# Two attention cores: the second head's probabilities are scaled on GpSimd, the first head's on VectorE

## The chip, the cores and the metric

The kernel runs on one core of one Trainium2 chip. The metric is the time of one execution on the device in microseconds (us). Engines are named as in the profile: PE is TensorE, DVE is VectorE, ACT is ScalarE, POOL is GpSimd, SP issues most of the transfers.

## The reference, cut to what matters

The program is two transformer stacks of two layers each on 256 tokens of width 1024, all in float32. Two of the four mixers are softmax attentions, and they alone are touched in what they compute with:

```python
def _sink_softmax(scores, sink):                 # first stack, layer 1: 16 heads, 256 queries, 512 keys
    m = max(sink, scores)                        # per query
    ex = [exp(s - m) for s in scores]
    denom = exp(sink - m) + sum(ex)
    return [e / denom for e in ex]               # then weights @ v

# second stack, layer 0 (mla_mixer): 16 heads, causal, 96-wide queries and keys, 64-wide values
    s = (qn . kn + qr . kr) * scale ; s = where(causal, s, MASK_VALUE)
    o = softmax(s) @ v
```

## The kernel before, in words

Each engine has its own instruction stream; semaphores tie them together. The streams are generated by one function, with one block for each engine. `stop >= 3` marks the first attention, `stop >= 5` the second, and both run through functions named `attention` (PE line 1120, DVE line 2305, ACT line 3059).

The first attention has 16 steps. Step n handles two heads (j = 0, 1) of one block of 128 queries: its scores are two banks of 128x512. The second attention has 8 steps of two heads; for each head there are 384 score columns, 256 for the later query block and 128 for the earlier one.

For step n the order is this. PE `score` writes two banks. DVE `most` masks them in place, takes the row maximum (line 2370, or 2495 and 2496) and makes the bias of the exponential. ACT `weights` makes the exponentials into `a_prob[:, n % 3, j, :]` with their row sums. DVE `normed` adds the sink's part (first attention only), takes the reciprocal of the sums (lines 2378, 2502) and scales the probabilities of both heads in place (helper `scale`, line 1788: one instruction for each head in the first attention, two for each head in the second), then raises `att_normed`. PE `turns_of` transposes the probabilities, head by head, into PS[0] and PS[1] (helper at line 646; 4 transposes a head, or 3). ACT copies each to SBUF (`att_copied`). PE `weigh` multiplies them with the values (line 1222, or 1330), and DVE copies the result out (line 2317, `att_taken`).

The steps are pipelined by hand. On PE, iteration s holds score(s), turns(s-2), weigh(s-3), in that order. On DVE it holds most(s), normed(s-1), the copy of s-3. On ACT it holds weights(s) and the two copies of s-1. PE line 1129 waits for `att_normed` before the turns of both heads.

GpSimd does nothing in either attention. Its stream goes from the sums of down-projection weights (line 3414) straight to a memset for the delta-rule mixer (line 3417). Two one-off semaphores of that mixer, `g_end_ready` (raised once, line 2572) and `g_half` (raised twice, line 2632), order VectorE's results before their readers on PE and ACT.

Of the kernel before, what the change touches and what calls it, by code (L numbers as in the profile page):

```python
# [106 lines left out]
def build(nc, A, out, stop=99):  # L107
    ctx = ExitStack()
    with ctx:
# [101 lines left out]
        for name in (  # L211
            "const_loaded", "vectors_loaded", "x_loaded", "phase_loaded", "rows_loaded", "packs_turned", "packs_copied",
            "cond_ready", "x_turned", "x_copied", "panel_used", "ada_ready", "ada_taken", "final_scaled",
            "square_ready", "sum_ready", "mean_ready", "rstd_ready", "scaled", "h_ready",
            "gu_ready", "silu_ready", "gu_taken", "out_ready", "out_taken", "proj_ready", "proj_taken",
            "dve_step", "act_step", "pool_step",
            "act_for_dve", "dve_for_act", "act_for_pe", "dve_for_pe", "pe_for_dve",
            "gates_split", "moved_ready", "moved_taken", "picks_ready", "most_ready", "acc_ready", "acc_step", "out_stored",
            "strip_exped", "strip_made", "mix_rows_made", "mix_rows_stored", "floor_cleared", "floor_moved", "mix_cols_ready",
            "mix_masked", "mix_exped", "unit_scored", "unit_weighed", "unit_valued", "num_taken", "ret_squared", "ret_summed",  # L220
            "den_ready", "y_spread", "y_scaled", "y_ready", "y_squared", "y_gated", "y_summed",
            "att_scored", "att_maxed", "att_exped", "att_normed", "att_turned", "att_copied", "att_out", "att_taken",
            "norm_squared", "norm_added", "norm_inverted", "norm_rooted", "norm_spread",
            "g_rows_ready", "g_stored", "g_spread", "g_masked", "g_decayed", "g_cols_turned", "g_cols_ready", "g_end_ready", "g_summed", "g_logs", "g_grown", "g_keyed",
            "g_paired", "g_compact", "g_level_masked", "g_turned", "g_u", "g_u_copied", "g_w", "g_diag", "g_half", "g_inverted",
            "g_tok_turned", "g_tok_copied", "scan_ready", "scan_u0", "scan_s", "scan_r", "scan_u1", "scan_out", "scan_squared",
            "g_scaled", "g_final_turned", "g_final",
            "tok_turned", "tok_copied", "sum_cleared",
            "blk_tokens", "blk_sums", "blk_act", "blk_copied", "blk_ready", "blk_taken", "blk_silu",
            "down_tokens", "down_sums", "down_first", "down_copied", "down_ready", "down_taken", "down_added",  # L230
            "final_copied",
            "att_rooted", "att_scaled", "rot_ready", "rot_taken", "heads_copied",
        ):
            s[name] = ctx.enter_context(nc.semaphore(name))
        mix_loaded = [ctx.enter_context(nc.semaphore(f"mix_loaded{i}")) for i in range(16)]
# [393 lines left out]
        def _(pe):  # L629
# [490 lines left out]
            def attention(N, first, score, turns_of, weigh):  # L1120

                for step in range(N + 3):
                    if step < N:
                        if step >= 2:
                            pe.wait_ge(s["att_exped"], first + step - 1)
                        score(step, 4 + 2 * (step % 2)).then_inc(s["att_scored"], 1)
                    if 0 <= step - 2 < N:
                        n = step - 2
                        pe.wait_ge(s["att_normed"], first + n + 1)
                        for j in range(2):  # L1130
                            if n:
                                pe.wait_ge(s["att_copied"], 2 * (first + n - 1) + j + 1)
                            turns_of(n, j, PS[j]).then_inc(s["att_turned"], 1)
                    if step - 3 >= 0:
                        n = step - 3
                        pe.wait_ge(s["att_copied"], 2 * (first + n + 1))
                        if n >= 2:
                            pe.wait_ge(s["att_taken"], first + n - 1)
                        weigh(n, PS[2 + n % 2]).then_inc(s["att_out"], 1)
# [202 lines left out]
            if stop >= 7:  # L1342
# [39 lines left out]
                for h in range(8):  # L1382
                    if h == 0:
                        pe.wait_ge(s["act_step"], 1 + 24)
                    elif h == 3:
                        pe.wait_ge(s["g_end_ready"], 1)
                    elif h in (4, 5):
                        pe.wait_ge(s["proj_taken"], c["proj"].n - 1)
                    elif h >= 6:
                        pe.wait_ge(s["g_paired"], h - 3)  # L1390
                    bank = PS[KEY_BANKS[h]]
                    for t in range(2):
                        v = slice(t * P, (t + 1) * P)
                        last = nc.tensor.matmul(bank[:, t * L:(t + 1) * L].rearrange("p (a n) -> p a n", a=2), g_x[:, 8 + h, v],
                                                g_x[:, h:h + 9:8, v], start=True, stop=True)
                    last.then_inc(s["g_keyed"], 1)
# [78 lines left out]
                    last.then_inc(s["g_w"], 1)  # L1475
                for g in range(2):
                    pe.wait_ge(s["g_diag"], g + 1)
                    pe.wait_ge(s["g_half"], g + 1)
                    for m in range(8 * g, 8 * g + 8):
                        last = product(PS[U_BANKS[g]], slice(64, P), m, g_pair[0:64, m // 2, m % 2, 1, 64:P], g_t1[0:64, m, :], 64)  # L1480
                    last.then_inc(s["g_u"], 1)
# [18 lines left out]
                for g in range(2):  # L1500
                    heads = range(4 * g, 4 * g + 4)
                    whole = lambda h: PS[h % 4]
                    outs = lambda h: PS[4 + 2 * g + h % 4 // 2][:, h % 2 * L:h % 2 * L + L]
                    pe.wait_ge(s["g_inverted"], g + 1)
                    for h in heads:
                        nc.tensor.matmul(whole(h)[:, 0:P], g_tt[:, 2 * h, :], g_v[:, h, 0, :], start=True, stop=True)\
                            .then_inc(s["scan_ready"], 1)
# [260 lines left out]
        def _(dve):  # L1768
# [4 lines left out]
            def link(ins):  # L1773

                ins.then_inc(s["dve_step"], 1)
                dve.wait_ge(s["dve_step"], c["step"].next())
# [9 lines left out]
            def scale(o, i, by, plus=None, op1=ALU.add):  # L1786
                if plus is None:
                    return V.tensor_scalar(o, i, by, None, ALU.mult)  # L1788
                return V.tensor_scalar(o, i, by, plus, ALU.mult, op1)
# [529 lines left out]
            if stop >= 3:  # L2319
# [54 lines left out]
                def normed(n):  # L2374

                    pair = slice(2 * n, 2 * n + 2)
                    link(tt(dsum[:, pair], dsum[:, pair], esink[:, pair], ALU.add))
                    link(V.reciprocal(rec[:, pair], dsum[:, pair]))
                    for j in range(2):
                        v = a_prob[:, n % 3, j, :]  # L2380
                        last = scale(v, v, rec[:, 2 * n + j:2 * n + j + 1])
                    return last

                attention(16, 0, most, normed, P, lambda n: hT[:, n // 2, (n % 2) * P:(n % 2 + 1) * P])
                add_project_out(1, 1, 5)
# [4 lines left out]
            if stop >= 5:  # L2390
# [108 lines left out]
                def normed_m(n):  # L2499

                    four = slice(4 * n, 4 * n + 4)
                    link(V.reciprocal(rec[:, four], dsum[:, four]))
                    for j in range(2):
                        for i, v in ((j, a_prob[:, n % 3, j, 0:L]), (2 + j, a_prob[:, n % 3, j, L:L + P])):
                            last = scale(v, v, rec[:, 4 * n + i:4 * n + i + 1])
                    return last

                attention(8, 16, most_m, normed_m, L, lambda n: hT[:, n, 0:L])
# [5 lines left out]
            if stop >= 7:  # L2514
# [54 lines left out]
                        V.tensor_copy(gcols, PS[7][:, 0:56]).then_inc(s["g_cols_ready"], 1)  # L2569
                dve.wait_ge(s["g_cols_turned"], 2)  # L2570
                dve.wait_ge(s["g_cols_ready"], 1)
                tt(small[:, G_DECAY:G_DECAY + 8], PS[7][:, 64:72], small[:, G_BIAS:G_BIAS + 8], ALU.add).then_inc(s["g_end_ready"], 1)

                def copy_gate(half, t):

# [49 lines left out]
                for g in range(2):  # L2625
                    dve.wait_ge(s["g_w"], 8 + g + 1)
                    bank = of(PS[W_BANKS[g]])
                    scale(group(g_t1, g)[32:64, :, 0:32], bank[32:64], -1.0)
                    for p in range(2):
                        r = slice(64 * p, 64 * p + 32)  # L2630
                        last = scale(group(g_tt, g)[r, :, 64 * p + 32:64 * p + 64], bank[r], -1.0)
                    last.then_inc(s["g_half"], 1)
                for g in range(2):
                    dve.wait_ge(s["g_w"], 10 + g + 1)
                    scale(group(g_tt, g)[0:64, :, 64:P], PS[W_BANKS[g]][0:64, :].rearrange("p (m n) -> p m n", m=8), -1.0)\
# [183 lines left out]
        def _(act):  # L2819
# [352 lines left out]
            if stop >= 7:  # L3172
# [19 lines left out]
                for b in range(24 + 2):  # L3192
# [10 lines left out]
                    if 3 <= b < 19:  # L3203
                        act.wait_ge(s["act_step"], c["step"].n - 1)
                        ac(g_sq[:, b - 3, :], g_x[:, b - 3, :], ACT.Square).then_inc(s["square_ready"], 1)
                act.wait_ge(s["g_end_ready"], 1)
                ac(small[:, G_DECAY:G_DECAY + 8], small[:, G_DECAY:G_DECAY + 8], ACT.Exp)
                ac(small[:, G_GROWN:G_GROWN + 16], small[:, G_ROWS:G_ROWS + 16], ACT.Exp).then_inc(s["g_grown"], 1)
                for h in range(8):
# [163 lines left out]
        def _(pool):  # L3373
# [26 lines left out]
            for j in range(1, 4):  # L3400
# [11 lines left out]
                if j > 1:  # L3412
                    pool.wait_ge(s["down_taken"], 10 * (j - 2) + 8)
                G.tensor_tensor(down_s4, down_weights(wa, 1), down_s2, ALU.subtract).then_inc(s["down_sums"], 1)
            if stop >= 7:
                pool.wait_ge(s["g_rows_ready"], 1)
                nc.gpsimd.memset(g_tt.rearrange("p m n -> p (m n)"), 0.0).then_inc(s["pool_step"], 1)  # L3417
# [109 lines left out]
```

## Time and profile before

| | us |
|---|---|
| median of 3 runs | 2345.54 |
| lowest, highest | 2343.82, 2351.57 |
| profiled execution, its own time | 2345.32 |
| its span in the profile | 2343.5 |
| PE busy | 2249.6 (96%) |
| VectorE busy | 1053.6 (45%) |
| ScalarE busy | 435.1 (19%) |
| GpSimd busy | 109.4 (5%) |

Times in the rows are microseconds from the span's start, or durations. In a timeline, one row can be several instructions of one kind that overlap or follow each other (x2, x8), with their joint duration. In brackets stands how long the engine was idle before and what released it. "mem" is SBUF, "banks" is PSUM. In a table of groups the last columns are: busy us in all, mean ns of one instruction, idle us before them. The first attention runs from about 940 to 1001, the second from about 1345 to 1376.

### The profile page before, as it was taken

What the parts mean: (1) busy time and instruction counts of PE and PEld (TensorE: products, weight loads), DVE (VectorE), ACT (ScalarE), POOL (GpSimd) and SP (SyncE); (2) the same over time, 40 slices, a digit from 0 to 9 for tenths busy, and PEclk for the clock granted to TensorE, in tenths of its full rate; (3) what the DMA queues carried; (4) which work ended last, traced back from release to release, by engine and by line L of the source; (5) the groups of instructions that cost most, each with busy time, mean ns of one, the idle gap of its engine ahead of it and who ended that gap; (6) DMA issues with size and microseconds to landing.
All of it is one profiled execution on the core that took longest, in us unless ns stands there. A gap on an engine that the chain in (4) does not pass through costs nothing.

```text
span 2343.5 us, 38868 instructions
## 1 busy us (share of the span) xinstructions
PE 2249.6 (96%) x16734; PEld 1629.6 (70%) x16734; DVE 1053.6 (45%) x2019; ACT 435.1 (19%) x1023; POOL 109.4 (5%) x103
## 2 busy tenths in 40 slices
PE   6999999999999999899999999999998989999997
PEld 4444454478885887588888678888775876666665
DVE  4586464488886346834432655450334420000001
ACT  3211251100000012720001241000332321111101
POOL 0210210000001220000000000000003000000000
PEclk8999999999999999999999999999999989999999
DMA  9334522245445223038884426886532258888894
GB/s 352 133 123 158 175 69 72 72 149 200 155 156 148 74 93 133 1 130 294 294 244 137 144 73 236 294 262 164 183 123 95 73 189 301 326 323 324 325 337 172
DMA packets 306216, 428.13 MB, mean 183 GB/s; under 512 B 11603, under 2 KB 166866, under 8 KB 305802
## 3 DMA queue, kind: packets, MB, share of 16 engines
q1 hardware_dynamic: 303412, 422.55, 52.9%
q10 hardware_dynamic: 2646, 3.26, 0.4%
q8 instruction: 125, 2.05, 0.4%
q14 instruction: 33, 0.27, 0.0%
HBM read 424.55 MB, written 1.13 MB: 182 GB/s over the span
## 4 chain that ended last, share of the span: by engine, by line
PE 90%; DVE 5%; ACT 2%; issue 1%; DMA 1%; SPq 1%; DVEq 0%; ACTq 0%
PE banks L637 76%; PE banks L891 3%; ACT mem L2821 2%; PE banks L646 1%; DVE mem L1795 1%; PE banks L1591 1%; PE banks L1000 1%; DVE mem L1788 1%; DVE mem L1792 1%; PE banks L1035 1%; DMA mem<-in_ada_w 1%; DVE mem L2370 1%; PE banks L1655 1%; PE banks L1422 1%; PE banks L855 1%
## 5 line engine op out<-in xcount | busy, mean ns | idle before, releaser
L637 PE MATMUL banks<-mem 128*32 128x128 f32 (+5 forms) x12660 | 1827.1, 360 | 22.9 <-ACT mem L2821 12.1
L637 PEld LDWEIGHTS banks<-mem 128*128 128x128 f32 (+3 forms) x12660 | 1309.4, 149 | 514.2 <-issue 312.2
L1792 DVE SCALAR_TENSOR_TENSOR mem<-mem 128x512 f32<-128x512 f32 (+5 forms) x509 | 366.6, 745 | 14.1 <-ACT mem L2821 4.5
L2821 ACT ACTIVATE mem<-banks 128x512 f32<-128x512 f32 (+8 forms) x367 | 145.9, 421 | 1126.3 <-PE banks L637 824.4
L2821 ACT ACTIVATE mem<-mem 128x256 f32<-128x256 f32 (+9 forms) x421 | 184.1, 490 | 662.3 <-DVE mem L1792 517.1
L1795 DVE TENSOR_TENSOR mem<-mem,banks 128x256 f32<-128x256 f32 (+3 forms) x88 | 43.1, 491 | 575.3 <-ACT mem L2821 548.7
L1792 DVE SCALAR_TENSOR_TENSOR mem<-banks,mem 128x256 f32<-128x256 f32 (+7 forms) x258 | 133.6, 543 | 341.5 <-PE banks L637 225.8
L1795 DVE TENSOR_TENSOR mem<-mem 128x256 f32<-128x256 f32 (+12 forms) x286 | 160.0, 569 | 36.2 <-ACT mem L2821 21.1
L1795 DVE TENSOR_TENSOR mem<-banks,mem 128x256 f32<-128x256 f32 (+3 forms) x223 | 90.5, 410 | 112.3 <-PE banks L637 61.4
L646 PE MATMUL banks<-mem 128*128 128x128 f32 (+3 forms) x396 | 64.0, 301 | 29.8 <-DMA mem<-in_ctx 11.3
L646 PEld LDWEIGHTS banks<-mem 128*128 128x128 f32 (+3 forms) x396 | 48.5, 155 | 57.2 <-issue 21.7
L891 PE MATMUL banks<-mem 128*128 128x256 f32 x320 | 75.6, 380 | 0.0
L2821 ACT ACTIVATE mem<-banks,mem 128x512 f32<-128x512 f32 (+4 forms) x110 | 55.3, 511 | 90.9 <-PE banks L637 59.8
L891 PEld LDWEIGHTS banks<-mem 128*128 128x128 f32 x320 | 60.9, 190 | 8.1
L2821 ACT ACT_TABLE_LOAD x41 | 52.6, 1283 | 25.3 <-issue 24.6
L3417 POOL MEMSET mem<- 128x2048 f32 x1 | 1.8, 1805 | 908.3 <-DVE mem L1792 908.3
L1792 DVE SCALAR_TENSOR_TENSOR mem<-mem,banks 128x256 f32<-128x256 f32 x88 | 35.3, 475 | 6.4 <-PE banks L735 6.4
L3407 POOL TENSOR_TENSOR mem<-mem 128x1408 f32<-128x1408 f32 x3 | 9.5, 3159 | 462.4 <-DMA mem<-in_ffn_w_out 418.7
L2328 DVE RECIPROCAL mem<-mem 128x512 f32<-128x512 f32 x6 | 20.1, 3352 | 22.6 <-ACT mem L2821 22.5
L3395 POOL TENSOR_TENSOR mem<-mem 128x256 f32<-128x256 f32 x32 | 22.6, 728 | 158.8 <-DMA mem<-mix_rows 158.6
L1000 PE MATMUL banks<-mem 64*128 64x256 f32 x192 | 27.0, 401 | 1.8 <-DVE mem L1792 1.6
L1591 PE MATMUL banks<-mem 128*128 128x192 f32 x128 | 25.8, 352 | 2.4 <-DVE mem L2745 2.4
(185 smaller groups left out, 820.9 us busy)
## 6 DMA issues: line engine op xcount, KB each, us to landing
mem<-in_ada_w SPq DMA_DIRECT2D x96, 1024.0 KB, 10.0
mem<-in_moe_w_gate_up SPq DMA_DIRECT2D x64, 1024.0 KB, 13.0
mem<-in_ffn_w_in SPq DMA_DIRECT2D x44, 1024.0 KB, 6.6
mem<-in_moe_w_down SPq DMA_DIRECT2D x48, 768.0 KB, 9.5
mem<-in_moe_w_gate_up SPq DMA_DIRECT2D x32, 768.0 KB, 12.7
mem<-in_ffn_w_out SPq DMA_DIRECT2D x32, 704.0 KB, 6.8
mem<-in_ffn_w_gate_up SPq DMA_DIRECT2D x22, 1024.0 KB, 6.7
mem<-in_ab_w_in SPq DMA_DIRECT2D x16, 1024.0 KB, 7.7
```

The lines of the kernel that those rows point to most:

```text
L637: ins = nc.tensor.matmul(o, lhsT, rhs, start=start, stop=stop)
L646: return nc.tensor.transpose(o, i, ident[0:n, 0:n])
L855: last = nc.tensor.matmul(bank, lhs[:, k, :], rhs[:, k, :], start=False, stop=k == KE_FF - 1, skip_group_check=True)
L891: last = nc.tensor.matmul(bank, a[:, k, :], b[:, k, :], start=False, stop=k == 3, skip_group_check=True)
L1000: last = nc.tensor.matmul(PS[2 * (n % 2) + j][:, i * L:(i + 1) * L], qk[r, first + 4 + p, key * P:(key + 1) * P], qk[r, first + p, q:q + L ...
L1035: nc.tensor.matmul(bank[j * HD:(j + 1) * HD, off + os.start:off + os.stop], mv[:, key, h * HD:(h + 1) * HD], mix_weights(h, u, d)[:, ws], ...
L1422: return nc.tensor.matmul(bank[into, (m % 8) * width:(m % 8 + 1) * width], lhsT, rhs, start=True, stop=True)
L1591: last = nc.tensor.matmul(bank[:, b * 2 * CAP:(b + 1) * 2 * CAP], h_tok[:, t, k * P:(k + 1) * P], pick[:, t, :], start=t == 0, stop=t == 1)
L1655: nc.tensor.matmul(moe_sum(4 * m + i), y_own[r, m, i % 2 * P:(i % 2 + 1) * P], back[r, e % 2, 0, :], start=False, stop=False, skip_group_c ...
L1792: return V.scalar_tensor_tensor(out=o, in0=a, scalar=sc, in1=b, op0=op0, op1=op1)
L1795: return V.tensor_tensor(o, a, b, op)
L2821: ac = lambda o, i, f, **k: nc.scalar.activation(o, i, f, **k)
```

## The change

The reciprocal of `normed` and `normed_m` raises a new semaphore `att_inverted`, on which both VectorE and GpSimd wait. VectorE then scales only head 0 and raises `att_normed`. GpSimd scales head 1 (one instruction of 128x512 a step in the first attention, one of 128x256 and one of 128x128 in the second) and raises a new semaphore `att_scaled_1`. PE waits for `att_normed` before the turns of head 0 and for `att_scaled_1` before those of head 1. To make room for two semaphores, `g_end_ready` becomes the second count of `g_cols_ready`, and `g_half` the first two counts of `g_inverted`.

```diff
@@ PE, attention @@
-                        pe.wait_ge(s["att_normed"], first + n + 1)
-                        for j in range(2):
+                        for j, scaled in enumerate(("att_normed", "att_scaled_1")):
+                            pe.wait_ge(s[scaled], first + n + 1)
                             if n:
                                 pe.wait_ge(s["att_copied"], 2 * (first + n - 1) + j + 1)
                             turns_of(n, j, PS[j]).then_inc(s["att_turned"], 1)
@@ DVE, normed @@
-                    link(V.reciprocal(rec[:, pair], dsum[:, pair]))
-                    for j in range(2):
-                        v = a_prob[:, n % 3, j, :]
-                        last = scale(v, v, rec[:, 2 * n + j:2 * n + j + 1])
-                    return last
+                    V.reciprocal(rec[:, pair], dsum[:, pair]).then_inc(s["att_inverted"], 1)
+                    dve.wait_ge(s["att_inverted"], n + 1)
+                    v = a_prob[:, n % 3, 0, :]
+                    return scale(v, v, rec[:, 2 * n:2 * n + 1])
@@ DVE, normed_m @@
-                    link(V.reciprocal(rec[:, four], dsum[:, four]))
-                    for j in range(2):
-                        for i, v in ((j, a_prob[:, n % 3, j, 0:L]), (2 + j, a_prob[:, n % 3, j, L:L + P])):
-                            last = scale(v, v, rec[:, 4 * n + i:4 * n + i + 1])
+                    V.reciprocal(rec[:, four], dsum[:, four]).then_inc(s["att_inverted"], 1)
+                    dve.wait_ge(s["att_inverted"], 16 + n + 1)
+                    for i, v in ((0, a_prob[:, n % 3, 0, 0:L]), (2, a_prob[:, n % 3, 0, L:L + P])):
+                        last = scale(v, v, rec[:, 4 * n + i:4 * n + i + 1])
                     return last
@@ POOL, before its work for the delta-rule mixer @@
+            if stop >= 3:
+                for n in range(16):
+                    pool.wait_ge(s["att_inverted"], n + 1)
+                    v = a_prob[:, n % 3, 1, :]
+                    G.tensor_scalar(v, v, a_mx[:, 4, 2 * n + 1:2 * n + 2], None, ALU.mult).then_inc(s["att_scaled_1"], 1)
+            if stop >= 5:
+                for n in range(8):
+                    pool.wait_ge(s["att_inverted"], 16 + n + 1)
+                    for i, v in ((1, a_prob[:, n % 3, 1, 0:L]), (3, a_prob[:, n % 3, 1, L:L + P])):
+                        last = G.tensor_scalar(v, v, a_mx[:, 4, 4 * n + i:4 * n + i + 1], None, ALU.mult)
+                    last.then_inc(s["att_scaled_1"], 1)
```

## Rows read from the trace of the kernel before

**Rows 1.** The page's head: the span of the profiled execution.

```profile
span 2343.5 us, 38868 instructions
```

**Rows 2.** Windows over the steady steps: busy, granted clock, DMA share, GB/s.

```profile
955.00:993.00 38.00, 35.68 (x315) 22.88 (x316) 36.06 (x103) 29.30 (x80) 0.00 (x0) 1.00 0.01 2
1357.00:1371.00 14.00, 12.82 (x90) 9.63 (x88) 13.55 (x47) 10.35 (x40) 0.00 (x0) 1.00 0.00 1
```

**Rows 3.** The chain that ended last, 957 to 962, its shares by line.

```profile
by line: DVE mem L1788 35.3%; DVE mem L2370 24.7%; DVE mem L1795 9.7%; DVE mem L2317 8.0%; DVE mem L2378 7.0%; DVE banks L1795 7.0%; DVE mem L1792 6.9%; issue 3.9%
```

**Rows 4.** Timelines of the first attention: start, duration, engine, instruction, idle before.

```profile
940.10 1.99 PE L1206 MATMUL banks<-mem 64*128 64x512 f32 x8
...
951.67 1.21 PE L646 MATMUL banks<-mem 128*128 128x128 f32 x8
951.79 0.43 DVE L1795 TENSOR_TENSOR banks<-banks,mem 128x256 f32<-128x256 f32 x1 [0.64 <-PE banks L1206]
...
954.18 0.88 DVE L1788 TENSOR_SCALAR mem<-mem 128x512 f32<-128x512 f32 x2
...
955.12 1.09 PE L646 MATMUL banks<-mem 128*128 128x128 f32 x8 [0.15 <-DVE mem L1788]
...
959.52 1.09 PE L1222 MATMUL banks<-mem 128*64 128x128 f32 x16
960.54 1.13 PE L1206 MATMUL banks<-mem 64*128 64x512 f32 x4
961.87 1.09 PE L646 MATMUL banks<-mem 128*128 128x128 f32 x8 [0.20 <-DVE mem L1788]
...
997.69 1.09 PE L646 MATMUL banks<-mem 128*128 128x128 f32 x8
```

**Rows 5.** Groups of instructions by form, 955 to 990: VectorE's scaling.

```profile
L1788 DVE TENSOR_SCALAR mem<-mem 128x512 f32<-128x512 f32 x21 | 9.3, 483 | 0.3
```

**Rows 6.** Timelines of the second attention.

```profile
1344.81 0.70 PE L1312 MATMUL banks<-mem 96*128 96x256 f32 x2 [0.84 <-DVEq L2485]
...
1346.22 0.60 PE L1312 MATMUL banks<-mem 96*128 96x256 f32 x2
...
1355.43 0.88 PE L646 MATMUL banks<-mem 128*128 128x128 f32 x6
...
1355.49 0.76 DVE L1795 TENSOR_TENSOR banks<-banks,mem 128x256 f32<-128x256 f32 x2
...
1357.03 0.70 PE L1312 MATMUL banks<-mem 96*128 96x256 f32 x2
...
1357.63 1.01 DVE L1788 TENSOR_SCALAR mem<-mem 128x256 f32<-128x256 f32 x4
...
1361.02 1.01 DVE L1788 TENSOR_SCALAR mem<-mem 128x256 f32<-128x256 f32 x4
```

**Rows 7.** Groups of instructions by form, GpSimd, the whole span.

```profile
L3423 POOL TENSOR_TENSOR mem<-mem 128x512 f32<-128x512 f32 x8 | 9.9, 1274 | 9.9 <-DMA mem<-decay_rows 9.9
...
L3442 POOL COPY mem<-mem 32x256 f32<-32x256 f32 x8 | 3.1, 394 | 0.3
L3417 POOL MEMSET mem<- 128x2048 f32 x1 | 1.8, 1805 | 908.3 <-DVE mem L1792 908.3
...
L3425 POOL MEMSET mem<- 128x1024 f32 x1 | 1.0, 951 | 1.0 <-ACT mem L2821 1.0
```

**Rows 8.** Timelines: VectorE and GpSimd beside each other, and alone.

```profile
55.62 10.34 DVE L1792 SCALAR_TENSOR_TENSOR mem<-mem 128x512 f32<-128x512 f32 x10
...
81.33 10.12 DVE L1792 SCALAR_TENSOR_TENSOR mem<-mem 128x512 f32<-128x512 f32 x14
...
1760.61 1.20 DVE L2581 TENSOR_SCALAR mem<-mem 128x8 f32<-128x8 f32 x1
...
1771.31 1.19 DVE L2594 COPY mem<-mem 32x256 f32<-32x256 f32 x4
...
1772.58 0.97 POOL L3431 TENSOR_TENSOR mem<-mem 128x256 f32<-128x256 f32 x1 [1.12 <-DVE mem L2594]
```

More of the change, by code:

```diff
@@ L223, in build @@
             "norm_squared", "norm_added", "norm_inverted", "norm_rooted", "norm_spread",
-            "g_rows_ready", "g_stored", "g_spread", "g_masked", "g_decayed", "g_cols_turned", "g_cols_ready", "g_end_ready", "g_summed", "g_logs", "g_grown", "g_keyed",
-            "g_paired", "g_compact", "g_level_masked", "g_turned", "g_u", "g_u_copied", "g_w", "g_diag", "g_half", "g_inverted",
+            "g_rows_ready", "g_stored", "g_spread", "g_masked", "g_decayed", "g_cols_turned", "g_cols_ready", "g_summed", "g_logs", "g_grown", "g_keyed",
+            "g_paired", "g_compact", "g_level_masked", "g_turned", "g_u", "g_u_copied", "g_w", "g_diag", "g_inverted",
             "g_tok_turned", "g_tok_copied", "scan_ready", "scan_u0", "scan_s", "scan_r", "scan_u1", "scan_out", "scan_squared",
@@ L231, in build @@
             "final_copied",
-            "att_rooted", "att_scaled", "rot_ready", "rot_taken", "heads_copied",
+            "att_rooted", "att_scaled", "rot_ready", "rot_taken", "heads_copied", "att_inverted", "att_scaled_1",
         ):
@@ L1385, in _ @@
                     elif h == 3:
-                        pe.wait_ge(s["g_end_ready"], 1)
+                        pe.wait_ge(s["g_cols_ready"], 2)
                     elif h in (4, 5):
@@ L1477, in _ @@
                     pe.wait_ge(s["g_diag"], g + 1)
-                    pe.wait_ge(s["g_half"], g + 1)
+                    pe.wait_ge(s["g_inverted"], g + 1)
                     for m in range(8 * g, 8 * g + 8):
@@ L1503, in _ @@
                     outs = lambda h: PS[4 + 2 * g + h % 4 // 2][:, h % 2 * L:h % 2 * L + L]
-                    pe.wait_ge(s["g_inverted"], g + 1)
+                    pe.wait_ge(s["g_inverted"], 2 + g + 1)
                     for h in heads:
@@ L2571, in _ @@
                 dve.wait_ge(s["g_cols_ready"], 1)
-                tt(small[:, G_DECAY:G_DECAY + 8], PS[7][:, 64:72], small[:, G_BIAS:G_BIAS + 8], ALU.add).then_inc(s["g_end_ready"], 1)
+                tt(small[:, G_DECAY:G_DECAY + 8], PS[7][:, 64:72], small[:, G_BIAS:G_BIAS + 8], ALU.add).then_inc(s["g_cols_ready"], 1)
                 def copy_gate(half, t):
@@ L2631, in _ @@
                         last = scale(group(g_tt, g)[r, :, 64 * p + 32:64 * p + 64], bank[r], -1.0)
-                    last.then_inc(s["g_half"], 1)
+                    last.then_inc(s["g_inverted"], 1)
                 for g in range(2):
@@ L3205, in _ @@
                         ac(g_sq[:, b - 3, :], g_x[:, b - 3, :], ACT.Square).then_inc(s["square_ready"], 1)
-                act.wait_ge(s["g_end_ready"], 1)
+                act.wait_ge(s["g_cols_ready"], 2)
                 ac(small[:, G_DECAY:G_DECAY + 8], small[:, G_DECAY:G_DECAY + 8], ACT.Exp)
```

## The prediction, made before the changed kernel was run

> **What bounds the kernel now.** I read the page first: a span of 2343.5 us [rows 1] in an execution of 2345.32, so 1.8 us lie around the span. Then I asked for the windows of the two attentions, because the change touches nothing else that takes time. In the steady steps of the first attention VectorE is busy 36.06 of 38 us and PE 35.68, in the second 13.55 and 12.82 of 14 [rows 2]. These are two engines at nearly the same load, so it matters which one ends each step. The chain of waits says it: between 957 and 962 every piece is VectorE's, 35.3% of it the scaling at line 1788 [rows 3]. PE stands idle for 0.20 us before the turns, released by that scaling; from 955.12 to 961.87 are two steps, 3.375 us each [rows 4]. The second attention has the same shape, 3.39 us a step (1357.63 to 1361.02) [rows 6]. The clock is at its upper level (1.00) in both windows and the DMA share 0.01 or less [rows 2]: no transfer is due, so the work behind an attention starts as much earlier as the attention ends earlier.
>
> **What is left when VectorE is relieved, first attention.** I call the start of PE's turns in iteration s T, and the start of VectorE's masking M.
> - PE alone: turns and weigh take 1.02 each (959.52 to 960.54 is one of them), a score 0.96 (two back to back take 1.99, of which some 0.07 is the pipeline's tail) [rows 4]. That is 3.00 us a step.
> - VectorE alone: 3.375 minus one scaling, which is 0.40 where two overlap (0.88 for two of 0.48) [rows 4, 5]: 2.98.
> - Across the engines, head 0: in the one iteration where VectorE waited for the scores, M is T + 0.12 (951.67, 951.79), the scaling begins 2.39 after M (954.18), takes 0.48, and PE starts 0.06 after the scaling's end (955.06, 955.12) [rows 4, 5]. So head 0 is ready at T + 3.05, and a step can't be shorter than 3.05.
> - Across the engines, head 1: GpSimd is released with VectorE by the reciprocal. The nearest row for its start is 0.08 after VectorE's end (1771.31 + 1.19 against 1772.58) [rows 8], while VectorE goes on 0.02 after its own reciprocal (its gaps are 3.9% of 5 us in the chain, some eight of them) [rows 3]; so VectorE's scaling goes first. If it keeps GpSimd out until it is done, GpSimd starts at M + 2.87 + 0.08. With X for its instruction and 0.06 to PE, head 1 is ready at T + 3.13 + X. Then PE has half the turns (0.51), a weigh (1.02) and a score (0.96) until the T two steps on. So two steps take 5.62 + X.
>
> **X, the price nobody has shown.** The trace has no tensor_scalar on GpSimd. Nearest is its one-input copy: 256 columns take 0.39, and a memset grows by 0.834 ns a column ((1805 - 951) / 1024) [rows 7]; for 512 columns 0.39 + 256 x 0.834 = 0.61. The far end is the two-input operation on the same 128x512: 1.27 [rows 7]. I take 0.61, since the scaling streams one tensor as the copy does; the operand of one column comes on top, unpriced. X = 0.61 gives 6.23 / 2 = 3.12 us a step, X = 1.27 gives 3.45. Below 0.48 head 0 bounds at 3.05. The step equals today's at X = 1.13.
> The Trainium skill (GPSIMD Engine Reference, section 3.1) gives 769 ns for 512 elements as the best case of a loop at 1.8 cycles an element; no run here shows it. By that figure a step would take 3.20 us and the 12 steps below would gain 2.1 in place of 3.1, an estimate from that page.
>
> **Sum, first attention.** M was bound to VectorE from 951.79 on, 12 steps of 3.375 until the last M at 992.3 [rows 4]. 12 x (3.375 - 3.12) = 3.1 us gained. At the end, the turns of the last step started at 997.69 [rows 4], 5.4 after the last M; now they start when turns(14) and one weigh are done. Head 1 of step 14 is ready at M + 3.0 + 0.61, its turns end at 4.1 and weigh(13) at 5.15: 0.2 gained. With X = 1.27 it is 12 x 0.07 = 0.8 lost, and 0.6 at the end. The first two steps lose nothing: there PE has a backlog at the lower clock level and finds both heads scaled. So +3.3, bounds -1.4 and (at 3.05) +4.3.
>
> **Second attention.** VectorE issues two scalings instead of four, 1.01 us for four [rows 6], so 0.46 to 0.50 less: about 2.93. PE: 1.60 for turns and weigh (1355.43 to 1357.03) and 1.41 for a score (1344.81 to 1346.22): 3.01 [rows 6]. GpSimd has 256 and 128 columns, 0.39 and 0.28, together 0.67 by the copy; by the two-input rate 0.73 and 0.46. Head 1: M is T + 0.06, the scaling starts at M + 2.14 [rows 6], two take 0.54, then 0.08 + 0.67 + 0.06: ready at T + 3.55; then 0.40 + 0.80 + 1.41, so 6.16 for two steps, 3.08 each. That would gain 0.31 a step.
> But here VectorE has a second scaling behind the first, and a waiting GpSimd may get in between. Then VectorE's second one waits 0.08 + 0.39, and the step is 3.40: nothing gained. Four steps are bound by VectorE in this way: 0 to 1.2 us. I take the middle, 0.6. At two-input rate without the intrusion it would gain 0.2, with it lose 4 x 0.35 = 1.4; the end adds 0 to -0.5.
>
> **What the trace says on sharing.** A VectorE tensor_scalar of 128x8 took 1.20 us beside GpSimd's 128x512 operations, though 128x512 takes 0.48 alone [rows 5, 8]: it waited for a whole GpSimd instruction. VectorE's two-input operations took 1.03 each beside GpSimd (10.34 for 10) and 0.72 alone (10.12 for 14) [rows 8]. The Trainium skill (SBUF — State Buffer, "Who interferes with whom") says that a tensor_scalar of VectorE in a 2-port mode and any GpSimd instruction exclude each other, whoever starts first. By that rule the trace's 1.20 agrees, and the two halves of the scaling would run one after the other and not together. My sum has it so by the row of 1.20; without any exclusion head 1 would be ready 0.5 earlier and head 0 would bound at 3.05.
>
> **The rest.** PE gains one wait for each step, behind which stand head 1's turns, the weigh and the next score: that is priced above. GpSimd waits in order from about 840 to 1373; behind it stands only the memset at line 3417, which was itself 908.3 us idle before [rows 7]. ScalarE copies each head when it is turned and is busy 29.30 of 38 [rows 2]. The merged semaphores add no instruction and keep the order of the same events: 0. Sum: 3.3 + 0.6 = 3.9 us; 2345.32 - 3.9 = 2341.4 for such an execution, and as the median stands 0.2 above the profiled one, 2341.6.
>
> **Rivals.**
> 1. GpSimd's scaling costs as much as its two-input work. This ends slower, from X = 1.13 on in the first attention: 1.4 lost there and between nothing and 1.9 in the second: 2347 to 2349. For it: an operand beside the stream. Against: one stream, and a copy at 0.39. Chance 0.25.
> 2. GpSimd gets the ports first, and VectorE's scaling waits for all of it. Head 0 is then ready at T + 0.12 + 2.37 + 0.08 + X + 0.54: 3.72 at X = 0.61, 4.38 at 1.27. 12 steps lose 4 to 12 us, the second attention 1 to 3: 2350 to 2361. For it: the 1.20 us row [rows 8]. Against: 0.02 against 0.08 us from release to start. Chance 0.10. (The Trainium skill, SBUF — State Buffer, "Who interferes with whom": whoever starts first holds the shared ports for its whole instruction; that rule would lead here if GpSimd started first.)
> 3. Dearer than any row, X near 2: 3.81 a step, 5.2 lost, 1 at the end, 3 in the second attention: 2355. Chance 0.07.
> 4. The engines hardly disturb each other: 3.05 in the first (3.9 + 0.4) and 3.01 in the second (4 x 0.38 + 0.3): 6.1 gained, 2339.4. This is as much as the change can give. Chance 0.07.
> 5. The steps get shorter and the kernel does not, because a later stage waits for its weights anyway: 2345.5. Against: DMA share 0.01 [rows 2]. Chance 0.03.
>
> **How the numbers follow.** The forecast has chance 0.48. A measurement of this kernel tells a change of 0.3%, 7 us, from none. No case gains 7 us: faster by more 0.02 (for what I have overlooked). Slower by more than 7 us are case 3 and the upper half of case 2, with a little of case 1: 0.10. Within: 0.88. The range holds the forecast and cases 1, 4 and 5, 0.83 together: 2339.4 to 2349, and I add 1 us at either end because three runs of the same kernel lay 1.7 below to 6 above their median: 2338.5 to 2350.
>
> **What would show it.** In the timeline the spacing of PE's turns: 3.12 (right), 3.375 or more (case 1), 3.7 and more with a VectorE scaling of over 1 us (case 2), 3.05 (case 4). GpSimd's rows give X and whether they start after VectorE's scaling ends. In the waits, PE's turns should be released by GpSimd and no longer by line 1788. In the second attention VectorE's second scaling shows whether GpSimd gets in between. The prediction is wrong if GpSimd's release takes much longer than 0.08 us, or if the wait moves to ScalarE.

## The result

| | median us | lowest, highest | runs |
|---|---|---|---|
| kernel before | 2347.32 | 2343.49, 2351.68 | 20 |
| changed kernel | 2351.38 | 2347.25, 2355.10 | 20 |

The changed kernel is slower: the ratio to the kernel before is 1.0017, with a 95% interval of 1.0011 to 1.0023, so 2.6 to 5.4 us. The forecast was 3.9 us faster. The profiled execution of the changed kernel took 2355.10 us, the slowest of its 20, with a span of 2353.3. Its span must not be subtracted from that of [rows 1]: 2.7 of the 9.8 us between them were already there when the first attention began (942.83 against 940.10), where the change does nothing. Another 2.0 lie between the two attentions (346.24 us against 344.20) and 2.4 behind the second (969.45 against 967.01). I put neither down to the change: over the eleven traces of this document these two stretches vary from 344.2 to 346.3 and from 966.7 to 971.5 us, and the one behind took 968.5 in a version in which GpSimd does nothing in the attentions (e7). What the change did is read inside the two attentions.

The page's head and its line of busy times; then windows over the same stretch as [rows 2] for the first attention and the matching one for the second (columns: us, PE, PEld, VectorE, ScalarE, GpSimd busy, granted clock, DMA share, GB/s):

```profile
span 2353.3 us, 38890 instructions
...
PE 2254.9 (96%) x16734; PEld 1628.7 (69%) x16734; DVE 1046.9 (44%) x1987; ACT 435.1 (18%) x1023; POOL 152.9 (6%) x135
```

```profile
955.00:993.00 38.00, 34.43 (x304) 21.49 (x304) 30.89 (x87) 27.85 (x74) 19.66 (x11) 1.00 0.01 1
1364.00:1378.00 14.00, 13.19 (x96) 9.79 (x92) 12.64 (x38) 10.79 (x41) 6.66 (x8) 1.00 0.00 1
```

VectorE was relieved as intended, from 36.06 to 30.89 us in the 38 of the first attention. But PE does less in the same time as well (35.68 to 34.43). A new wait has taken the place of the old one. The groups by form show the price of what was moved (last columns: busy us, mean ns of one, idle us before):

```profile
L3418 POOL TENSOR_SCALAR mem<-mem 128x512 f32<-128x512 f32 x16 | 29.7, 1857 | 133.3 <-DVE mem L2378 133.3
...
L3423 POOL TENSOR_SCALAR mem<-mem 128x256 f32<-128x256 f32 x8 | 8.7, 1084 | 365.6 <-DVE mem L2501 365.6
...
L3423 POOL TENSOR_SCALAR mem<-mem 128x128 f32<-128x128 f32 x8 | 4.8, 601 | 0.0
```

GpSimd's scaling takes 1.86 us. The two-input operation on the same shape, which the prediction took as the far end, takes 1.27 [rows 7]. The chain of waits, first its shares by line over 957 to 992, then one turn of the loop (start, length, what):

```profile
by line: POOL mem L3418 26.7%; DVE mem L2370 17.7%; PE banks L1206 15.5%; PE banks L1222 13.7%; PE banks L646 9.4%; DVE banks L1795 6.3%; issue 3.5%; DVE mem L1795 3.5%; DVE mem L2378 2.5%; DVE mem L1792 2.5%
...
962.13 0.66 PE banks L646 x4
962.78 1.02 PE banks L1222 x16
963.81 1.08 PE banks L1206 x4
...
964.91 0.44 DVE banks L1795
...
965.38 1.24 DVE mem L2370
...
966.84 0.24 DVE mem L1795 x2
...
967.10 0.18 DVE mem L2378
...
967.36 1.87 POOL mem L3418
...
969.27 0.66 PE banks L646 x4
```

In [rows 3] every piece is VectorE's. Here the chain goes from PE's turns of head 1 over the weigh and the score to VectorE's maximum and reciprocal, to GpSimd, and back to the turns of head 1 two steps later. That circle takes 7.14 us (962.13 to 969.27), where two steps took 6.75 in [rows 4]. PE shows it too: in the steps that close the circle, which is every second one, head 0 is turned at once and head 1 waits for GpSimd.

```profile
966.84 1.13 PE L1206 MATMUL banks<-mem 64*128 64x512 f32 x4
967.90 0.66 PE L646 MATMUL banks<-mem 128*128 128x128 f32 x4
969.27 0.66 PE L646 MATMUL banks<-mem 128*128 128x128 f32 x4 [0.71 <-POOL mem L3418]
969.86 1.09 PE L1222 MATMUL banks<-mem 128*64 128x128 f32 x16
970.88 1.13 PE L1206 MATMUL banks<-mem 64*128 64x512 f32 x4
971.94 1.09 PE L646 MATMUL banks<-mem 128*128 128x128 f32 x8
972.97 1.09 PE L1222 MATMUL banks<-mem 128*64 128x128 f32 x16
```

**Where the time is.** I cut each attention at PE's turns: the fill up to the fourth iteration's turns (at 951.67 in the kernel before, 953.55 in the changed one), the steady steps from there to the last turns that follow a score (992.26 and 996.49), and the tail up to the next projection.

| us, profiled executions | first: 12 steady steps | per step | tail | second: 4 steady steps | per step | tail |
|---|---|---|---|---|---|---|
| before | 40.59 | 3.38 | 8.35 | 13.42 | 3.36 | 7.64 |
| changed | 42.94 | 3.58 | 9.01 | 13.61 | 3.40 | 7.92 |

The sum is 2.35 + 0.66 + 0.19 + 0.28 = 3.5 us, inside the measured 2.6 to 5.4. The fill of the first attention went the other way in this pair of executions, 10.72 us against 11.57: PE's fourth score took 1.13 us, in the kernel before 2.08, at a granted clock of 0.50. This is not the change's doing. With GpSimd at work e1 has the short fill (10.72) and e8 the long one (11.58), and e7, in which GpSimd does nothing there, has 10.71. So I leave the fill out of the sum.

### The profile page after: what moved, and what is told of

Its sections match the earlier page's. It is cut to its first block, busy times and chain, and to the rows that moved or that the text cites. A ratio compares the mean times of both kernels' runs of the same rounds, so it can differ in the third digit from the quotient of the medians.

```text
span 2353.3 us, 38890 instructions
## 1 busy us (share of the span) xinstructions
PE 2254.9 (96%) x16734; PEld 1628.7 (69%) x16734; DVE 1046.9 (44%) x1987; ACT 435.1 (18%) x1023; POOL 152.9 (6%) x135
## 3 DMA queue, kind: packets, MB, share of 16 engines
q10 hardware_dynamic: 2646, 3.26, 0.4%
HBM read 424.55 MB, written 1.13 MB: 181 GB/s over the span
## 4 chain that ended last, share of the span: by engine, by line
PE 91%; DVE 4%; ACT 2%; issue 1%; DMA 1%; POOL 1%; SPq 1%; DVEq 0%; ACTq 0%
PE banks L637 76%; PE banks L891 3%; ACT mem L2820 1%; PE banks L646 1%; DVE mem L1795 1%; PE banks L1591 1%; PE banks L1000 1%; DMA mem<-in_ada_w 1%; DVE mem L1792 1%; PE banks L1035 1%; PE banks L1655 1%; PE banks L1422 1%; PE banks L855 1%; POOL mem L3418 1%; SPq L492 1%
## 5 line engine op out<-in xcount | busy, mean ns | idle before, releaser
L3418 POOL TENSOR_SCALAR mem<-mem 128x512 f32<-128x512 f32 x16 | 29.7, 1857 | 133.3 <-DVE mem L2378 133.3
L3423 POOL TENSOR_SCALAR mem<-mem 128x256 f32<-128x256 f32 (+1 forms) x16 | 13.3, 842 | 365.6 <-DVE mem L2501 365.6
```

The costliest lines, as they stand in the source:

```text
L3418: G.tensor_scalar(v, v, a_mx[:, 4, 2 * n + 1:2 * n + 2], None, ALU.mult).then_inc(s["att_scaled_1"], 1)
```

## The experiments

Each kernel ran on one chip together with the kernel before; "ratio" is to that, with its 95% interval. e1, e5 and e8 were executed once each, so only their traces are read. Steps, fill and tail are cut as above. The code is cut to the lines that matter and shows the first attention; the second has the matching edit.

**e1: GpSimd starts only after VectorE's scaling.** How much of 1.86 us is the instruction, how much is waiting for VectorE?

```diff
-                    pool.wait_ge(s["att_inverted"], n + 1)
+                    pool.wait_ge(s["att_normed"], n + 1)
```

> The changed kernel, but GpSimd waits until VectorE has scaled head 0 (att_normed) instead of for the reciprocal (att_inverted), so that the two scalings never overlap. In the changed kernel GpSimd's 128x512 scaling took 1.86 us from 0.06 after VectorE's start. Theory 1 (the instruction itself costs 1.86 us): it takes 1.86 again, starts 0.45 later, and two steps take 7.15 + 0.45 = 7.6 us. Rival (0.4 of the 1.86 is waiting for VectorE's scaling of 0.49): it takes 1.4 to 1.45, ends where it ended before, and two steps take 7.15 to 7.25 us.

```profile
L3418 POOL TENSOR_SCALAR mem<-mem 128x512 f32<-128x512 f32 x16 | 25.0, 1565 | 139.9 <-DVE mem L1788 139.9
```

Alone it takes 1.57 us, between the two expectations: 0.29 of the 1.86 is the overlap with VectorE, the rest is its own. For 256 and 128 columns it takes 926 and 605 ns here, so 2.5 ns for each column and 0.29 fixed. The steps took 3.69 us (3.58 in the changed kernel): GpSimd now starts 2.96 after VectorE's masking began, 0.51 later than in the changed kernel, and gets 0.29 of it back. Two steps took 7.39, between the 7.15 to 7.25 and the 7.6 expected. With this instruction, then, letting both start at once is right, and the price is what is wrong.

**e2: VectorE scales both heads.** Everything of the diff but GpSimd: does the split wait or the merging of semaphores cost anything?

```diff
-                    v = a_prob[:, n % 3, 0, :]
-                    return scale(v, v, rec[:, 2 * n:2 * n + 1])
+                    v = a_prob[:, n % 3, 0, :]
+                    scale(v, v, rec[:, 2 * n:2 * n + 1]).then_inc(s["att_normed"], 1)
+                    v = a_prob[:, n % 3, 1, :]
+                    return scale(v, v, rec[:, 2 * n + 1:2 * n + 2])      # raises att_scaled_1
```

> All of the change but GpSimd: VectorE scales both heads and raises att_normed after head 0 and att_scaled_1 after head 1; the split wait on PE and the merged semaphores stay. Theory 1 (the loss is GpSimd's chain and nothing else): steps of 3.375 us as before the change, ratio to the kernel before 0.9995 to 1.0000. Rival (the rest of the change costs the 1.5 us of the measured 4 that the two attentions don't show): ratio 1.0004 to 1.0010.

Measured: 2345.13 against 2347.50 us, ratio 0.9994 (0.9985 to 1.0003), steps of 3.35 and 3.30 us. The rest of the change (the split wait, the merged semaphores) costs nothing that can be measured, so the loss is GpSimd's part.

**e3: the weigh leaves the loop.** PE turns head 1 after the weigh of the step before, not ahead of it (the edit in words):

```diff
-    score(s); turns of head 0 of s-2; turns of head 1 of s-2; weigh(s-3)
+    score(s); turns of head 0 of s-2; weigh(s-3); turns of head 1 of s-2
```

> The changed kernel, but PE turns head 1 only after the weigh of the step before: score(s), turns of head 0 of s-2, weigh(s-3), turns of head 1 of s-2. Theory 1 (a loop over two steps through GpSimd, 4.5 us from T to head 1 ready and then half the turns, a weigh and a score): the weigh leaves the loop, which falls from 7.15 to 6.1 for two steps; PE itself bounds at 3.05 to 3.15 us a step; first attention 3 us shorter than before the change, second about 1.4 shorter, ratio to the kernel before 0.9978 to 0.9985. Rival (ScalarE, whose copy of head 1 now comes later and stands ahead of its next exponentials, becomes late): steps of 3.3 us and more, ratio 0.9995 to 1.0015.

```profile
965.26 1.13 PE L1210 MATMUL banks<-mem 64*128 64x512 f32 x4
966.32 0.66 PE L646 MATMUL banks<-mem 128*128 128x128 f32 x4
966.91 1.09 PE L1226 MATMUL banks<-mem 128*64 128x128 f32 x16
967.93 0.66 PE L646 MATMUL banks<-mem 128*128 128x128 f32 x4
968.52 1.13 PE L1210 MATMUL banks<-mem 64*128 64x512 f32 x4
...
by line: PE banks L646 35.8%; PE banks L1226 32.2%; PE banks L1210 32.0%
```

The last line is the chain of waits from 957 to 992: every piece of it is PE's. The same GpSimd instruction, still 1857 ns, no longer holds up a step. The step is 3.26 us and no row of PE has idle time ahead of it, so PE is the bound. That confirms the loop. I expected 3.05 to 3.15 and had set PE's floor too low for this order: two groups of turns take 0.59 each where one takes 1.02, and a score takes 1.06. The rival's ratio came true, 1.0001 (0.9992 to 1.0010), but not its mechanism, since PE waits neither for ScalarE nor for anything else. The trace says where the gain went: the steady steps gain 1.5 us in the first attention (39.09 against 40.59) and 0.9 in the second (12.54 against 13.42), and the two tails lose 1.0 and 0.6. The 0.7 us that are left are too few for the ratio to show.

**e4: the two-input form.** GpSimd multiplies with the column of reciprocals repeated along the row.

```diff
-                    G.tensor_scalar(v, v, a_mx[:, 4, 2 * n + 1:2 * n + 2], None, ALU.mult)
+                    G.tensor_tensor(v, v, a_mx[:, 4, 2 * n + 1:2 * n + 2].to_broadcast([P, T2]), ALU.mult)
```

> The changed kernel, but GpSimd scales with the two-input tensor_tensor, the second operand being the column of reciprocals repeated along the row. Theory 1 (price of the form of the instruction; the trace has 1.27 us for tensor_tensor on 128x512): it takes 1.27 to 1.3, two steps take 6.55 us, ratio to the kernel before 0.9993 to 1.0000. Rival (both forms cost the same beside VectorE, because waiting for the shared ports makes up the 1.86): 1.8 and more, ratio 1.001 or above.

The timeline of one step:

```profile
965.35 1.36 DVE L1788 TENSOR_SCALAR mem<-mem 128x512 f32<-128x512 f32 x1
965.40 1.04 POOL L3418 TENSOR_TENSOR mem<-mem 128x512 f32<-128x512 f32 x1 [2.82 <-DVE mem L2378]
...
966.77 1.09 PE L646 MATMUL banks<-mem 128*128 128x128 f32 x8 [0.68 <-DVE mem L1788]
```

Neither expectation held in its mechanism. The form is cheaper than any expected (1.04 us), and the kernel is the slowest of all: ratio 1.0043 (1.0028 to 1.0059), 3.84 us a step. VectorE's own scaling takes 1.36 us in place of 0.49. This is rival 2 of the prediction, in a form it did not foresee: VectorE starts 0.05 us before GpSimd and waits for it all the same. It ends 0.27 us after GpSimd. VectorE's streaming of 512 columns would take just that, at the 0.52 ns a column by which its group of 128x256 in the second attention (mean 350 ns) and that of 128x512 (483 [rows 5]) differ. So it looks as if VectorE had its fixed part behind it and streamed only when GpSimd was done; no row shows that directly.

**e5: both edits, two inputs and after VectorE.**

> Both edits of e1 and e4: GpSimd scales with the two-input form and starts only when VectorE has scaled head 0. Theory 2 (two separate prices: the form costs 1.04 us on GpSimd and 1.57 for tensor_scalar; and what overlaps pays extra, 0.29 on GpSimd's side for tensor_scalar, 0.87 on VectorE's side for the two-input form): VectorE's scaling is back at 0.49, GpSimd's stays 1.04, head 1 is ready 4.06 after VectorE's masking began, and with 2.68 for half the turns, a weigh and a score two steps take 6.75 us, 3.37 a step. Rival (the 1.04 of e4 was short because GpSimd held the ports from before VectorE, and the form costs 1.3 or more otherwise): 1.27 and more, 3.5 a step.

```profile
966.24 0.49 DVE L1788 TENSOR_SCALAR mem<-mem 128x512 f32<-128x512 f32 x1
...
966.80 1.04 POOL L3418 TENSOR_TENSOR mem<-mem 128x512 f32<-128x512 f32 x1 [2.44 <-DVE mem L1788]
```

VectorE's scaling is back at 0.49 and GpSimd's stays at 1.04: the price of the instruction and the obstruction are separate. The step is 3.42 us, close to the 3.37 expected and no better than the 3.38 before the change.

**e6: GpSimd takes half of head 1.** 256 of 512 columns in the first attention, the piece of 128 in the second; VectorE does the rest.

```diff
-                    v = a_prob[:, n % 3, 1, :]
+                    v = a_prob[:, n % 3, 1, 0:L]                          # GpSimd
+                    scale(v, v, rec[:, 2 * n:2 * n + 1]).then_inc(s["att_normed"], 1)
+                    v = a_prob[:, n % 3, 1, L:T2]                         # VectorE, after head 0
+                    return scale(v, v, rec[:, 2 * n + 1:2 * n + 2])
```

> The changed kernel, but GpSimd scales only half of head 1 in the first attention (256 of 512 columns) and only the 128-column piece of head 1 in the second; VectorE scales the rest after head 0, and the turns of head 1 wait for both. Theory 2 (the loop over two steps is GpSimd's price plus 5.2): GpSimd takes 1.1 to 1.25 for 256 columns, its loop falls to 3.2 a step, VectorE with 0.27 more is at 3.25 and sets the step; first attention 1.5 us shorter than before the change, second 0.5 to 1.0; ratio to the kernel before 0.9987 to 0.9996. Rival (VectorE's own scalings are held up by GpSimd's when there are several of them in a row, 0.77 instead of 0.54 for two in the second attention): VectorE's two take 1.0 and more in place of 0.75, steps of 3.38 to 3.5, ratio 1.0000 to 1.0010.

```profile
965.11 0.97 DVE L1790 TENSOR_SCALAR mem<-mem 128x512 f32<-128x512 f32 x2
965.17 1.22 POOL L3424 TENSOR_SCALAR mem<-mem 128x256 f32<-128x256 f32 x1 [2.25 <-DVE mem L2380]
...
L1790 DVE TENSOR_SCALAR mem<-mem 128x256 f32<-128x256 f32 x11 | 6.3, 570 | 0.0
```

GpSimd takes 1.22 us for 256 columns (0.93 alone, in e1, and 0.29), as expected. VectorE takes 0.97 for its two where 0.75 were due (0.40 and 0.35). It is the second that pays: 570 ns in place of 350, while its first keeps 488. So the rival was right: 3.45 us a step, ratio 1.0000 (0.9991 to 1.0009). In the second attention the step is 3.26, a little better than the 3.36 before.

**e7: relieve VectorE of something else.** No GpSimd; the split wait of e2; ScalarE copies each result out of PSUM.

```diff
-                        V.tensor_copy(place(n), PS[2 + n % 2][:, 0:width]).then_inc(s["att_taken"], 1)     # VectorE, n = step - 3
+                        ac(place(n), PS[2 + n % 2][:, 0:out_width], ACT.Copy).then_inc(s["att_taken"], 1)  # ScalarE, n = step - 3
```

> GpSimd does nothing, VectorE scales both heads with the split wait (as in e2), and the copy of each step's result out of PSUM (line 2317) goes from VectorE to ScalarE, between its exponentials and its copies of the turned heads. Theory 2 (what bounds the steps before the change is VectorE's 3.375 us, and what takes over is the loop M to head 1 to M two steps on, 3.27 + 0.06 + 3.0 = 6.35, or PE with 3.11): a step of 3.17 to 3.2 us in the first attention and about 3.1 in the second, 2.3 and 1.3 us less than before the change, ratio to the kernel before 0.9980 to 0.9988. Rival (ScalarE, busy 2.6 of 3.375 us a step and 0.3 more now, becomes late for the exponentials): steps of 3.3 and more, ratio 0.9995 or above.

```profile
966.92 0.88 DVE L1788 TENSOR_SCALAR mem<-mem 128x512 f32<-128x512 f32 x2
...
967.46 1.09 PE L646 MATMUL banks<-mem 128*128 128x128 f32 x8
967.72 0.43 DVE L1795 TENSOR_TENSOR banks<-banks,mem 128x256 f32<-128x256 f32 x1
...
by line: DVE mem L2366 38.8%; DVE mem L1788 27.7%; DVE banks L1795 11.1%; DVE mem L1795 8.1%; DVE mem L2374 5.6%; DVE mem L1792 5.4%; issue 3.7%
```

2342.82 against 2345.82 us, ratio 0.9987 (0.9978 to 0.9997): the one version here whose gain is clear of noise. The step is 3.18 us, and 3.07 in the second attention, as expected. The chain of waits from 957 to 992 (the last line) is still VectorE's throughout, but its step is 0.20 shorter; 0.03 of that is there without the moved copy (3.35 in e2).

**e8: a constant for the column.** Does the operand make GpSimd's tensor_scalar dear? As e1, but head 1 is multiplied by 0.5 and so not normalised.

> As e1 (GpSimd starts after VectorE's scaling, nothing overlaps), but GpSimd multiplies head 1 by the constant 0.5 in place of the column of reciprocals, so head 1 isn't normalised. Theory a (the operand that is a column of SBUF makes tensor_scalar dear): the 128x512 instruction falls from 1.57 us towards the copy's 0.61. Theory b (tensor_scalar on GpSimd costs 2.5 ns a column whatever its scalar is): 1.45 to 1.57 us.

```profile
L3418 POOL TENSOR_SCALAR mem<-mem 128x512 f32<-128x512 f32 x16 | 23.8, 1488 | 141.1 <-DVE mem L1788 141.1
```

1.49 us in place of 1.57: the column costs 0.08 and is not what makes the instruction dear. Why a tensor_scalar on GpSimd costs this much stays open.

**e9: the price that the prediction assumed.** GpSimd copies head 1 onto itself, with the waits of the changed kernel; head 1 is not normalised.

> The changed kernel with its own waits, but GpSimd copies head 1 onto itself and doesn't scale it, so head 1 isn't normalised. This gives the instruction the price that the prediction assumed. If that price was the only thing wrong in it: the copy takes 0.6 to 0.9 us, the loop through GpSimd falls to 3.0 to 3.1 a step, and the bound is head 0 or PE, 3.05 to 3.12 us a step in the first attention; 3.1 to 3.9 us less than before the change there, 0.5 to 1.5 less in the second; ratio to the kernel before 0.9978 to 0.9988. Rival (the two engines in each other's way cost as much as the price, as in e4, where VectorE's scaling took 1.36 in place of 0.49): VectorE's scaling of 0.8 us and more, steps of 3.3 us or more, ratio 0.9995 or above.

```profile
967.34 0.92 DVE L1788 TENSOR_SCALAR mem<-mem 128x512 f32<-128x512 f32 x1
967.37 0.61 POOL L3418 COPY mem<-mem 128x512 f32<-128x512 f32 x1 [2.80 <-DVE mem L2378]
...
968.32 1.09 PE L646 MATMUL banks<-mem 128*128 128x128 f32 x8 [0.24 <-DVE mem L1788]
...
1361.77 0.80 DVE L1788 TENSOR_SCALAR mem<-mem 128x256 f32<-128x256 f32 x2
1361.80 0.69 POOL L3423 COPY mem<-mem 128x256 f32<-128x256 f32 x2 [2.48 <-DVE mem L2501]
```

The copy takes 0.61 us, exactly the figure of the sum, and the kernel is not measurably faster: ratio 1.0003 (0.9995 to 1.0012), 3.40 us a step. VectorE's scaling takes 0.92 and ends 0.28 after GpSimd, as in e4. VectorE is the bound again, with 0.40 saved and 0.43 given back. So the price was not the only thing wrong. In the second attention (the last two rows) VectorE takes 0.80 where it took 1.01 [rows 6], and there the step falls from 3.36 to 3.18.

## Why the prediction was wrong

**What held.** VectorE was the bound, and its scaling released PE's turns [rows 3, 4]. The loop over two steps was the right structure, and so were its terms: VectorE's masking 0.11 after PE's turns begin (964.80 to 964.91), the scaling 2.39 after that (964.91 to 967.30 in the changed kernel), PE 0.04 after GpSimd's end. With X = 1.57 (e1) the sum's 5.62 + X gives 7.19 for two steps; measured 7.14. That this is so close is partly luck. The sum let GpSimd wait for all of VectorE's scaling and start 0.56 behind its start; it started 0.06 behind and took 0.29 longer for it. Half the turns took 0.58 where 0.51 stood and the score 1.06 where 0.96 stood, 0.17 more. The two errors nearly cancel. The merged semaphores and the split wait cost nothing measurable (e2). And the 3.5 us found inside the attentions leave nothing of size to a later stage.

**The step that failed: "X, the price nobody has shown".** It was put at 0.61 us by the nearest one-input row, with 1.27 as the far end. The instruction takes 1.57 alone and 1.86 in place. The argument "one stream, like the copy" was the fault: a copy and a multiplication by a scalar both stream one tensor, yet cost 0.83 (from 256 to 512 columns) and 2.5 ns a column on this engine (e9, e1). The two-input row was no bound either, since the two-input form is the cheaper one for this very work (1.04, e4). The break-even was named at X = 1.13, and rival 1, slower from X = 1.13 on, is the mechanism that decided, with its own price too small: it was bounded at 2349, and the measured median is 2351.38. Rival 3 came closest in price (X near 2, at 0.07).

**A second step would have failed as well: "VectorE's scaling goes first".** It was read from start times, 0.02 us against 0.08. In the changed kernel it came true by the instruction chosen: VectorE keeps its 0.49 and GpSimd pays 0.29. With a copy (e9) or the two-input form (e4) VectorE's row starts first too, by 0.03 to 0.05 us, and VectorE then ends after GpSimd's whole instruction. Rival 2 had the right consequence (its estimate of 3.72 us a step at X = 0.61 was 3.40 in e9, because VectorE streams only 0.27 after GpSimd and not all of 0.48 anew) and the wrong condition. Had X been 0.61, the 3.9 us would still not have come: in the trace of e9 the steady steps of the first attention gain nothing (40.76 us against 40.59), and the second attention gains 0.7 in its steps and 0.2 in its tail.

The Trainium skill (SBUF — State Buffer, "Who interferes with whom") says that whoever issues first has the shared ports for its whole instruction, and that the other is blocked for so long. In e4 and e9 the runs agree that VectorE's one scaling lasts until GpSimd's whole instruction is over, and differ on the order, if a row's start is taken for the issue: the engine whose row starts first is the one that waits. What a row gives as the start need not be the moment when the ports are taken, and I did not find out when that is. Where GpSimd's tensor_scalar meets the second of two VectorE scalings, the wait is not for a whole instruction: in e6 the second one takes 0.57 in place of 0.35 and is over at 966.08, while GpSimd works until 966.39.

**The range.** It reached 2350.0, from cases that bounded X at 1.27, and it was laid around a median of three runs, 2345.54; over 20 runs the kernel before has 2347.32. Both errors point the same way. A loss of 3.5 to 4.1 us on the first base is 2349.0 to 2349.6 and would have lain inside; on 2347.32 it doesn't. There is a slip in the chances as well: case 3 and the upper half of case 2 are 0.12, where 0.10 was put for them.

**The second attention.** The prediction had 0 to 1.2 us gained, depending on whether GpSimd gets between VectorE's two scalings.

```profile
1364.58 0.77 DVE L1788 TENSOR_SCALAR mem<-mem 128x256 f32<-128x256 f32 x2
...
1364.63 1.67 POOL L3423 TENSOR_SCALAR mem<-mem 128x256 f32<-128x256 f32 x2 [1.42 <-DVE mem L2501]
```

They took 0.77 us in place of 0.54, so it does get in the way, but by 0.23 and not by a whole instruction. With 1.67 us for GpSimd's two pieces in place of 0.67, the step went from 3.36 to 3.40. With pieces of 0.69 (e9) it was 3.18, so here the price was what mattered.

## What to carry to other kernels

Before work is moved to another engine, price the very instruction on the very engine: a row of another opcode with the same number of streams was off by 2.6 times here, and a row with more streams was no upper bound. Find the loop that the moved work closes and count over how many steps it runs: an engine idle for half of the time still set the pace, because its 1.86 us lay in series with PE's turns, weigh and score and with VectorE's work from the masking to the reciprocal. Ask too whom the moved instruction holds up while it runs: even at the price assumed, the 0.40 us taken from VectorE came back as 0.43 us of waiting (e9). And a busy engine can be relieved of another piece: 0.28 us of copying from PSUM given to ScalarE brought what 0.40 us of scaling given to GpSimd did not, as it went to an engine that had slack (busy 29.30 of 38 us before [rows 2]) and that no wait of the new loop turned out to hang on.

## What was new of the hardware

- GpSimd, 128 partitions, float32, alone: tensor_scalar with a column 1.57 us for 512 elements, 0.93 for 256 and 0.61 for 128 (e1), and with a constant 1.49 for 512 (e8); tensor_tensor with its second operand repeated along the row 1.04, 0.61 and 0.40 (e5); copy 0.61, 0.40 and 0.35 for the same lengths, measured beside VectorE's scaling (e9). The Trainium skill (GPSIMD Engine Reference, section 3.1) has 769 ns as the best case of a loop over 512 elements; the trace of e1 has twice that for tensor_scalar.
- VectorE's tensor_scalar of 128x512 and a GpSimd instruction hold each other up, and the GpSimd instruction decides who pays. With GpSimd's tensor_scalar it is GpSimd (1.86 in place of 1.57). With its copy or tensor_tensor it is VectorE (0.92 and 1.36 in place of 0.49), which ends 0.27 to 0.28 after GpSimd. VectorE's row starts first in all three. With 256 columns beside the copy, in the second attention of e9, VectorE ends 0.14 after GpSimd (0.57 in place of 0.35).
- The second of two VectorE scalings in a row pays about 0.22 beside GpSimd's tensor_scalar and ends before it: 128 columns 0.50 in place of 0.28 (the changed kernel), 256 columns 0.57 in place of 0.35 (e6).
- The granted clock's fall to 0.50 and its return in the fill of the first attention come at a different place of the work from one execution to the next. The fill took 11.57 us where the fourth score still ran at the lower level (2.08 us, the kernel before; e8 has 11.58) and 10.72 where it ran at the upper (1.13 us, the changed kernel; e1, e3, e6 and e7 have 10.71 to 10.73). In e2 and e5 the clock changed within the scores (1.52 and 1.64 us for the fourth), and the fill took 10.39 and 10.38. Long and short fills were seen with GpSimd at work and without. In e4 and e9 PE waited for VectorE's longer scaling there (1.29 and 0.56 us), and 11.59 and 11.07 are not the clock's alone.
